# A hybrid decoder step on one core: the first burst of cached keys, the turn of v and the last norm chain change places

## What is computed

```python
h = rms_norm(x, norm_mix_pre[l])
u = h @ w_in[l]
hq, hf, hi, hgate, dq, dk, dv, g_hg, g_da = jnp.split(u, IN_SPLIT_POINTS, axis=-1)
...
o_hg, s_new = hgrn2_recurrence(hq, hf, hi, lb, s0)        # 8 heads, 128 x 128 states
o_hg = rms_norm(o_hg.astype(x.dtype), hg_norm_w[l]) * jax.nn.silu(hgate)
y_hg = o_hg.reshape(b, L, HG_WIDTH) @ w_branch_hg[l]
...
o_da = diff_attend(q, k_all, v_all, q_pos, k_pos, rel_bias_table, lam)   # 2 softmax maps a head
o_da = rms_norm(o_da.astype(x.dtype), da_subln_w[l]) * (1.0 - lam_init)
y_da = o_da.reshape(b, L, DA_WIDTH) @ w_branch_da[l]
mixed = (jax.nn.sigmoid(g_hg) * y_hg + jax.nn.sigmoid(g_da) * y_da) @ w_out[l]
```

## Time and profile before

| what | value |
|---|---|
| median of three runs | 1884.2 us |
| profiled execution, its own time | 1886.4 us |
| span of that execution | 1884.9 us |
| PE, ACT, DVE, POOL busy | 99%, 43%, 57%, 7% |
| stretch of the eight rounds | from about 185 us to about 805 us of the span |
| DMA, mean over the span | 236 GB/s; 304 to 383 GB/s in the page's slices of the rounds |
| granted TensorE clock, mean | 0.998 |

### The profile page before, as it was taken

One profiled execution on the slowest core, in us unless ns is written; L12 is line 12 of the kernel. 1 busy time (PEld: TensorE's weight loads), 2 busy tenths in 40 slices (PEclk: granted clock), 3 DMA queues, 4 the chain that ended last, 5 costly groups with the idle time before them and its releaser, 6 DMA issues.

```text
span 1884.9 us, 39626 instructions
## 1 busy us (share of the span) xinstructions
PE 1863.8 (99%) x15318; PEld 1772.6 (94%) x15318; DVE 1069.2 (57%) x1440; ACT 811.3 (43%) x1075; POOL 133.0 (7%) x172
## 2 busy tenths in 40 slices
PE   9999999999999999899999999999999999999998
PEld 9999888888888888699999999999999999999998
DVE  8443667566665676565547754544554445545555
ACT  6333535435444354454445433333333334445454
POOL 1023121011110110100000000000000000000000
PEclk9999999999999999999999999999999999999999
DMA  8877989989999999777544555445454454544541
GB/s 317 182 257 228 375 338 357 383 342 368 352 362 371 371 369 351 304 277 249 189 154 148 164 160 160 153 154 178 157 165 152 155 173 157 165 158 155 168 156 57
DMA packets 125183, 444.38 MB, mean 236 GB/s; under 512 B 15749, under 2 KB 19861, under 8 KB 125056
## 3 DMA queue, kind: packets, MB, share of 16 engines
q1 hardware_dynamic: 112720, 402.31, 59.7%
q0 software_dynamic: 11168, 39.72, 7.2%
q10 hardware_dynamic: 1232, 1.47, 0.2%
HBM read 423.50 MB, written 22.54 MB: 237 GB/s over the span
## 4 chain that ended last, share of the span: by engine, by line
PE 94%; DMA 2%; DVE 2%; issue 1%; ACT 1%; POOL 0%; ACTq 0%; DVEq 0%; SPq 0%; POOLq 0%
PE ps L447 49%; PE ps L436 6%; PE ps L438 6%; PE ps L437 6%; PE ps L1871 5%; PE ps L1873 5%; PE ps L1872 5%; PE ps L979 3%; PE ps L1008 3%; PE ps L1513 3%; DMA raw<-w_in 1%; DMA gates<-uT 0%; DMA uT<-stage 0%; DVE w_lo L372 0%; PE ps L752 0%
## 5 line engine op out<-in xcount | busy, mean ns | idle before, releaser
L372 DVE TENSOR_TENSOR w_lo<-raw,w_hi 128x1024 fp32r<-128x1024 f32 x416 | 510.8, 1243 | 453.7 <-ACT w_hi L367 240.3
L367 ACT ACTIVATE w_hi<-raw 128x1024 fp32r<-128x1024 f32 x236 | 245.8, 1055 | 363.8 <-PE ps L447 302.1
L1871 PE MATMUL ps<-hid_hi,w_hi 128*128 128x320 f32 x680 | 203.4, 299 | 0.0
L1872 PE MATMUL ps<-hid_hi,w_lo 128*128 128x320 f32 x680 | 203.3, 299 | 0.0
L1873 PE MATMUL ps<-hid_lo,w_hi 128*128 128x320 f32 x680 | 203.3, 299 | 0.0
L395 ACT ACTIVATE w_hi<-raw 128x1024 fp32r<-128x1024 f32 x124 | 128.0, 1051 | 148.2 <-DMA raw<-w_in 134.1
L447 PE MATMUL ps<-x_hi,w_hi 128*128 128x320 f32 x1200 | 191.0, 303 | 0.1
L447 PEld LDWEIGHTS ps<-x_hi,w_hi 128*128 128x128 f32 x1200 | 169.3, 189 | 10.9 <-issue 7.2
L447 PE MATMUL ps<-x_hi,w_lo 128*128 128x320 f32 x1136 | 177.5, 299 | 0.0
L447 PE MATMUL ps<-x_lo,w_hi 128*128 128x320 f32 x1072 | 167.5, 299 | 0.0
L447 PEld LDWEIGHTS ps<-x_hi,w_lo 128*128 128x128 f32 x1136 | 161.9, 189 | 0.0
(11 more groups left out here) (365 smaller groups left out, 3102.9 us busy)
## 6 DMA issues: line engine op xcount, KB each, us to landing
raw<-w_in SPq DMA_DIRECT2D x176, 512.0 KB, 8.2
raw<-w_up SPq DMA_DIRECT2D x176, 512.0 KB, 3.5
raw<-ck SPq DMA_DIRECT2D x128, 512.0 KB, 6.4
raw<-cv SPq DMA_DIRECT2D x128, 512.0 KB, 7.0
raw<-w_dn SPq DMA_DIRECT2D x88, 512.0 KB, 3.5
raw<-w_out SPq DMA_DIRECT2D x32, 512.0 KB, 4.3
uT<-stage POOLq DMA_DIRECT2D x14, 640.0 KB, 7.9
raw<-w_hg SPq DMA_DIRECT2D x16, 512.0 KB, 5.9
```

The costliest lines, as they stand in the source:

```text
L367: act.activation(w_hi[slot % HALVES][:, :], raw[slot][:, :], ACT.Copy).then_inc(hi_ready, 1)
L372: dve.tensor_tensor(w_lo[half][:, :], raw[slot][:, :], w_hi[half][:, :].bitcast(F32), ALU.subtract).then_inc(lo_ready, 1)
L1871: pe.matmul(ps[:, m, 0:T], wh[:, c], xh, **dict(add, start=q == 0))
L1872: pe.matmul(ps[:, m, 0:T], wl[:, c], xh, **add)
```

## The change

The key pages of the first burst come directly behind A0 in `ROUND`, ahead of A1, and PE takes the burst directly behind `new_scores`. v of the next head is turned at the end of a round, behind `turn_back`, and its copy on ACT (`tok`) stands there too. The banks of prompt scores, of v and of the turned probabilities are exchanged: scores in banks 4 and 6, v in 5, `pd_t` in 4. So "i_t" now waits for "s", "pd_t" for "st2", and the second burst no longer for `pdt`. In the last round ACT's "sq" waits for the head's output and `ds_s` and stands ahead of D2 hi; POOL's sum ("ss") stands ahead of the stores of the states; "rt" stands directly behind D2 hi; DVE reads the last gate set (L554) ahead of D1 lo.

```diff
-ROUND = (items("A", 0, 2) + BURSTS[0] + items("A", 2, 6) + BURSTS[1] + items("A", 6, 8) + items("D", 0, 4)
+ROUND = (items("A", 0, 1) + BURSTS[0] + items("A", 1, 6) + BURSTS[1] + items("A", 6, 8) + items("D", 0, 4)
...
-        k_pool = Steps(sem("k_pool"), "zero ss", 1)
+        k_pool = Steps(sem("k_pool"), "ss", 1)
...
+        def act_v(act, h):
+            h_act.begin()
+            act.wait_ge(h_pe.sem, h_pe.at(h, "vk"))
+            h_act.done(act.activation(v_tok[:, :, :], ps[:, 5, 0:2 * P].rearrange("p (c d) -> p c d", c=2), ACT.Copy), "tok")
...
             if q == 1:
-                h_act.begin()
                 act.wait_ge(set_out, 4 * hg_set(h) + 2)
                 act.wait_ge(h_pool.sem, h_pool.last(h - 1))
                 h_act.done(act.activation(kin[:, :], x[:, 1, :], ACT.Sigmoid), "ef")
-                act.wait_ge(h_pe.sem, h_pe.at(h, "vk"))
-                h_act.done(act.activation(v_tok[:, :, :], ps[:, 6, 0:2 * P].rearrange("p (c d) -> p c d", c=2),
-                                          ACT.Copy), "tok")
...
+        def v_by_token(pe, h):
+            h_pe.begin()
+            pe.wait_ge(head_landed, HEAD_LOADS * (h + 1))
+            pe.sem_inc(passed, 1)
+            for j in range(2):
+                ins = pe.transpose(ps[:, 5, j * P:(j + 1) * P], mv[:, j * P:(j + 1) * P], ident[:, :])
+            h_pe.done(ins, "vk")
...
                 pe.wait_ge(h_vec.sem, h_vec.at(h, "i_smp"))
-                pe.wait_ge(h_act.sem, h_act.at(h, "tok"))
+                pe.wait_ge(h_vec.sem, h_vec.at(h, "s"))
                 h_pe.done(to_tokens(x[:, 2, :], i_smp[:, :, :, :], 6), "i_t")
...
             if q == 5:
-                pe.wait_ge(h_vec.sem, h_vec.at(h, "aT"))
+                pe.wait_ge(h_vec.sem, h_vec.at(h, "st2"))
                 for j in range(3):
-                    ins = pe.transpose(ps[:, 5, j * P:(j + 1) * P], pd[:, j * P:(j + 1) * P], ident[:, :])
+                    ins = pe.transpose(ps[:, 4, j * P:(j + 1) * P], pd[:, j * P:(j + 1) * P], ident[:, :])
...
             elif what == "sq":
-                act.wait_ge(h_vec.sem, h_vec.last(r))
+                act.wait_ge(h_vec.sem, h_vec.at(r, "o"))
+                act.wait_ge(h_pe.sem, h_pe.last(r))
...
-                k_vec.done(dve.tensor_tensor(s_all[:, :, HALF:], ps[:, 4:6, 3 * P:3 * P + NQ], near[:, :, PAGE:], ALU.add), "new")
+                for m in range(2):
+                    ins = dve.tensor_tensor(s_all[:, m, HALF:], ps[:, 4 + 2 * m, 3 * P:3 * P + NQ], near[:, m, PAGE:], ALU.add)
+                k_vec.done(ins, "new")
...
                 pe.wait_ge(k_act.sem, k_act.at(r, "g0"))
-                pe.wait_ge(h_act.sem, h_act.at(r, "pdt"))
                 pe.sem_inc(passed, 1)
             else:
-                pe.wait_ge(h_vec.sem, h_vec.at(r, "s"))
+                pe.wait_ge(h_act.sem, h_act.at(r, "tok"))
...
             round_hi(act, r + 1, "A", 0)
             act_pages(act, r, "o")
+            act_v(act, r + 1)
...
             act_pages(act, r, "p")
+            act_pages(act, r, "sq")
             round_hi(act, r, "D", 2)
-            act_pages(act, r, "sq")
+            act_pages(act, r, "rt")
             act_pages(act, r, "p0")
             act_pages(act, r, "pn")
             round_hi(act, r, "D", 3)
-            act_pages(act, r, "rt")
...
             round_lo(dve, r, "D", 0)
+            read_set(dve, gate_set(r), 1, SETS_U + 2 + r)
             round_lo(dve, r, "D", 1)
-            read_set(dve, gate_set(r), 1, SETS_U + 2 + r)
...
-                if q in (1, 5):
+                if q in (0, 5):
                     scores(pe, r, q // 4)
...
             turn_back(pe, r)
+            v_by_token(pe, r + 1)
...
             store_set(pool, gate_set(r), 1, GATE + 4 * r)
+            k_pool.begin()
+            if isinstance(r, int):
+                square_sums(pool, r)
             pool_head(pool, r)
```

More of the change, by code:

```diff
@@ L301, in build @@
         h_pe = Steps(sem("h_pe"), "vk scores i_t kd_t a ds pd_t o_s0 pv o ds_s", 1)
-        h_act = Steps(sem("h_act"), "ef tok lg eG p i_tok kd_tok pdt i_smp o_att", 1)
+        h_act = Steps(sem("h_act"), "tok ef lg eG p i_tok kd_tok pdt i_smp o_att", 1)
         h_vec = Steps(sem("h_vec"), "i_smp fg kin s max nmax G Gd qk qkd rc rcl pd2 pd aT st1 mid st2 own o s_three s_new", 1)
@@ L310, in build @@
         v_n_landed = sem("v_n_landed")
+        v_n_zero = sem("v_n_zero")
         k_pe = Steps(sem("k_pe"), "new h0 s0 h1 s1", 1)
-        k_pool = Steps(sem("k_pool"), "zero ss", 1)
+        k_pool = Steps(sem("k_pool"), "ss", 1)
         k_act = Steps(sem("k_act"), "q silu g0 g1 p sq rt rt_da", 1)
@@ L593, in act_head @@
                 act.wait_ge(h_pe.sem, h_pe.at(h, "pd_t"))
-                h_act.done(act.activation(pdt[:, :, :], ps[:, 5, 0:3 * P].rearrange("p (c d) -> p c d", c=3),
+                h_act.done(act.activation(pdt[:, :, :], ps[:, 4, 0:3 * P].rearrange("p (c d) -> p c d", c=3),
                                           ACT.Copy), "pdt")
@@ L635, in vec_head @@
                     close = mb[:, m, :]
[L636 removed]
+                    dve.scalar_tensor_tensor(s_at[:, m, 0:P], ps[:, 4 + 2 * m, 0:P], SCALE, close[:, P:2 * P],
                                              ALU.mult, ALU.add)
[L638 removed]
+                    ins = dve.scalar_tensor_tensor(s_at[:, m, P:3 * P], ps[:, 4 + 2 * m, P:3 * P], SCALE, close,
                                              ALU.mult, ALU.add)
@@ L730, in pe_head @@
             if q == 0:
-                h_pe.begin()
-                pe.wait_ge(head_landed, HEAD_LOADS * (h + 1))
                 pe.wait_ge(v_vec.sem, v_vec.last(h - 1))
-                for j in range(2):
-                    ins = pe.transpose(ps[:, 6, j * P:(j + 1) * P], mv[:, j * P:(j + 1) * P], ident[:, :])
-                h_pe.done(ins, "vk")
                 for m in range(2):
                     own_q, own_k = mq[DH * m:DH * m + DH, :], mk[DH * m:DH * m + DH, :]
-                    pe.matmul(ps[:, 4 + m, 0:P], own_q[:, 0:P], own_k[:, 0:P], start=True, stop=True)
-                    ins = pe.matmul(ps[:, 4 + m, P:3 * P], own_q[:, P:SEQ], own_k[:, 0:SEQ], start=True, stop=True)
+                    pe.matmul(ps[:, 4 + 2 * m, 0:P], own_q[:, 0:P], own_k[:, 0:P], start=True, stop=True)
+                    ins = pe.matmul(ps[:, 4 + 2 * m, P:3 * P], own_q[:, P:SEQ], own_k[:, 0:SEQ], start=True, stop=True)
                 h_pe.done(ins, "scores")
@@ L952, in new_scores @@
                         h, own, rows = 2 * j + e, slice(DH * m, DH * m + DH), own_rows(1, e)
-                        ins = pe.matmul(ps[32 * j:32 * j + 32, 4 + m, 3 * P:3 * P + NQ], q_rows[own, h, rows], k_own[own, h, :],
+                        ins = pe.matmul(ps[32 * j:32 * j + 32, 4 + 2 * m, 3 * P:3 * P + NQ], q_rows[own, h, rows], k_own[own, h, :],
                                         start=e == 0, stop=e == 1)
@@ L1173, in pe_last, with square_sums @@
             turn_back(pe, r)
+        def square_sums(pool, r):
+            pool.wait_ge(k_act.sem, k_act.at(r, "sq"))
+            pool.sem_inc(passed, 1)
+            k_pool.done(pool.partition_all_reduce(sq_all[:, :], n_sq[:, :], channels=P, reduce_op=bass.bass_isa.ReduceOp.add), "ss")
         def pool_round(pool, r):
@@ L1182, in pool_round @@
             pool.sem_inc(stage_free, 1)
-            k_pool.begin()
-            k_pool.done(pool.memset(v_new[:, :], 0.0), "zero")
-            pool.wait_ge(k_pool.sem, k_pool.at(r, "zero"))
+            pool.memset(v_new[:, :], 0.0).then_inc(v_n_zero, 1)
+            pool.wait_ge(v_n_zero, r + 1)
             pool.sem_inc(passed, 1)
@@ L1188, in pool_round @@
                 bass.ds(r, 1)].rearrange("a q d -> (a q) d")).then_inc(v_n_landed, 16)
-            pool.wait_ge(k_act.sem, k_act.at(r, "sq"))
-            pool.sem_inc(passed, 1)
-            k_pool.done(pool.partition_all_reduce(sq_all[:, :], n_sq[:, :], channels=P, reduce_op=bass.bass_isa.ReduceOp.add), "ss")
+            if not isinstance(r, int):
+                square_sums(pool, r)
             pool.wait_ge(head_stored, HEAD_STORES * (r + 1))
@@ L1991, in _ @@
             act.wait_ge(new_v_stored, 16)
+            act.wait_ge(bias_stored, 16)
+            act_v(act, 0)
             with act.Fori(0, LAST) as r:
@@ L2113, in _ @@
             pe.wait_ge(new_v_kept, 2)
+            v_by_token(pe, 0)
             with pe.Fori(0, LAST) as r:
@@ L2121, in _ @@
             pool.sem_inc(h_pool.sem, 1)
-            pool.sem_inc(k_pool.sem, 2)
+            pool.sem_inc(k_pool.sem, 1)
             pool.sem_inc(stage_free, 2)
```

## The result

| | before | after |
|---|---|---|
| median | 1884.18 us (1882.97 to 1884.62, 6 runs) | 1891.36 us (1889.85 to 1892.97, 6 runs) |
| profiled execution, its own time | 1886.44 us | 1889.85 us |
| its span | 1884.9 us | 1888.3 us |

The changed kernel is **slower by 0.38%**: ratio 1.0038, 95% interval 1.0028 to 1.0049. The forecast was 1887.4 us, its range 1876 to 1892: the median lies inside the range, 4.0 us above the forecast. In microseconds the two medians are 7.2 apart, with an interval of 5.3 to 9.2, where the forecast had 3.2.

The account below looks back on a forecast made before the run. PE was taken to bound the kernel, busy 1863.8 of 1884.9 us. Rounds +11.4 - 1.5 - 0.5 = +9.4 us, last round -6.2, sum +3.2: 1887.4 us against the median of 1884.2, range 1876 to 1892.

Parts of the forecast that it names:

- t + 15.5 us: Rounds 1 to 7: `ds` can start 15.5 us after A1 hi's start t, through ACT's and DVE's in-order work.
- The term of 11.4 us: Later `ds` summed over rounds 1 to 7: 11.4 us lost, bounds 0 and 15; round 1 worst, round 3 best.
- The first rival: Rounds 1 to 7: chain behind A1 hidden, rounds cost only PE's own, total 1876.4 us; chance 0.22.
- the burst's join: First burst behind `new_scores`: one entry to and one return from small tiles saved, 0.30 us a round.
- the rival "saves nothing": First burst: one block saves nothing, `ds` absorbs it in rounds 1 to 7, 0.3 us lost: 1887.7; no chance given.
- the second burst: Second burst of each round: its wait for ACT's `pdt` goes, 0.21 us a round, 1.5 over rounds 1 to 7.
- the last round: Last round: earlier norm roots cut the wait ahead of D3; `turn_back` moves from 803.61 to 797.4, -6.2 us.
- the rival that POOL holds the chain: Last round: the norm chain is held by POOL, +2.5 us, total 1889.9; chance 0.08.
- the prediction's last estimate: Last round on DVE: a small sum of the division would be held by POOL's sum for about 1.1 us.
- The slower rival: First value page: sum over partitions catches D4's remainder in four more rounds, +6.6 us, total 1894; chance 0.10.
- v a round ahead: v's transposes behind `turn_back`, ACT's copy ahead of A1 hi: costs 0, or 0.4 us if uncovered.
- "s" for "i_t": Bank exchange: "i_t" waits for "s", which ends near 435.2, before PE arrives at 436.1; no cost unless late.

Follow-up runs that it names:

- the two pairs: Kernel before and changed kernel, both unedited, each profiled twice and compared execution by execution; the parts of the shift sum to +6.0 and +5.9 us.
- the halving: Changed kernel with four of a burst's eight key waits ahead of it and four ahead of its second half: 1890.42 us, ratio 1.0044 to the kernel before.
- all repairs: Changed kernel with the head's elementwise work ahead of A1's split, key waits by half, rows' copy between branch granules: 1877.33 us, 1876.67 us when repeated.

## Why the prediction was right, and where it fell short

**Right: what decides.** The prediction picked the load order, worked out that A1's late landing makes `ds` late by the elementwise chain on ACT and DVE, and set t + 15.5 us. Rounds 1 to 7 of both profiles, 14 in all, lie between 15.28 and 15.50. The term of 11.4 us measured 12.1 and 11.1. Only the sum agrees so well: single rounds lie between +1.0 and +2.6 us, and the same round differs by up to 0.9 us between the two executions, so that round 3, forecast as the best with 1.3, lost 2.3 in the first. Moving the head's work off that chain took the median from 1891.36 to 1881.58 and in the profile 7.8 us from these seven rounds: shown by experiment. The first rival, the chain hidden, is out. Its price was wrong too: with the chain out of the way the kernel took 1881.58 us and not 1876.4, for the reason that follows.

**Wrong by size: the burst's join, -0.30 us a round.** In round 0, where nothing behind is late, the step from `new_scores` to "kd_t" costs +0.42 and +0.41 us in the two pairs. I counted an entry and a return saved, and nothing for PE's queue. Joining saves 0.17 us behind "i_t" (0.20 to the burst before, 0.03 to A2 now) and 0.02 of the return (1.19 us before, 1.17 now, behind the transposes): 0.19 and not 0.30. Against it, the burst starts 0.61 us later behind `new_scores` than A1 did (0.88 against 0.27). `new_scores` is 32 matmuls of 8 columns and over in 0.27 us, which covers few of the burst's eight key waits; A1 and the transposes had covered them all (0.20 us from the last transpose to the burst). With four waits the cost is +0.2 instead of +0.4 us in rounds 0 to 6: shown by the halving in three profiles. What the rest of the 0.61 us is made of, no run here shows. Only round 0 pays in the changed kernel (+0.8 against the forecast, with the 0.1 of its second burst); elsewhere `ds` absorbs it, as the rival "saves nothing" said.

**Wrong by size: the second burst, -0.21 us a round.** It measured 0.06 to 0.12 in the first pair (0.28 in round 7). The row "<- ACT pd, 0.2" names what PE waited for last; right beneath lie the key waits, shown by the halving. That is some 0.6 us over seven rounds. Another 0.3 is that behind a wait for `kd_tok` the stretch from `ds` to "pd_t" takes 7.07 us instead of 7.02. Together the term is +0.8 to +1.0 us off.

**Right: the last round**, -6.2 us by way of ACT's second branch granule. It stood at 796.26 before and at 805.52 after; the rounds had moved by 9.3, so it moved by 0.0 of its own where I had -0.4, and `turn_back` gained 6.0 us in the first pair, 4.9 in the second (before's second execution was itself quicker there). Alone it gave 4.7 us in the median, with an interval of 2.8 to 6.8. The sum over partitions began (782.15) as D1's remainder ended, which took its usual 1.24 us; the rival that POOL holds the chain is out. A small addition of the division (L928) ran inside the sum and took 0.28 us instead of 0.16, so it was held for 0.1 us where the prediction's last estimate had about 1.1.

**Right by luck: the profiled execution.** The forecast for it was 1889.6 us, and it took 1889.85; the spans differ by 3.4 us where the forecast had 3.2. The table shows what that is made of: +6.0 of the change, and -3.4 of stalls at the first value page that did not come back. The same program a second time had 1.4 us of them instead of 3.3. In the medians, where such chance evens out, the 3.2 us stand against 7.2. So what the forecast lacked is 2.7 to 2.8 us by the table (join 0.8, second burst 0.8 to 1.0, and the rest in landings or in the last round), and 1.2 us or so that no row places.

**The slower rival**, the sum catching D4's remainder in four more rounds, did not come: waits for `p_keys` 0 and 2 times. **v a round ahead** and **"s" for "i_t"** cost nothing, as said: no wait of PE names `v_tok` or `s_at` in either profile.

## What to carry over

When a load moves back in the order, find the first instruction on each in-order engine that waits for it and walk the work behind it to the next consumer: here a load set back by eight slots cost some 1.7 us a round through ACT and DVE, and taking independent work out from behind it gave 1.1 of that back. Count the semaphore waits on PE's queue where the matmuls ahead are short, above all in a loop, and spread them over the work that needs them. Price a wait of PE by the distance between two starts, not by the idle time in the view, which was a quarter too small here (6.4 against 8.5 us). Compare a change of a few tenths of a percent by two profiles of each kernel, since one of them can hold several microseconds of stalls that are nobody's.

## What the runs showed of the hardware

- **Semaphore waits that hold nothing up by themselves cost time on PE's queue when the work before them is short**: in the looped rounds four fewer gave 0.2 us back, at the first burst (0.85 to 0.65 us) and at the second (0.75 to 0.56). In the round that is written out, eight and four waits gave the same at the second burst (0.57 and 0.56).
- **The granted clock fell behind short idle times in some rounds only**: with A1 loaded first it fell to half behind 1.85 and 1.83 us of waiting for keys (rounds 3 and 5) and stayed at full behind 1.81, 1.98 and 1.85 (rounds 2, 6 and 7), and the 2.57 us ahead of `turn_back` left it at full in the changed kernel's profile. No run here separates what the difference is.
- **The sum over partitions holds DVE's remainder, an operation with two SBUF inputs, until 2.3 us behind the sum's start, and not for its whole 3.55 us.** In the kernel before, remainders that began 1.26 and 1.56 us behind the start took 2.30 and 2.00 us instead of 1.2, and one that began 2.66 us behind it took 1.23. One that began up to 0.33 us ahead of the sum was held as well (3.88 us, all repairs, round 0; 3.70 and 3.75 in the kernel before). From 0.37 us ahead on it was not, and the sum took longer instead: 4.32, 4.01 and 3.89 us behind remainders that began 0.37, 0.68 and 0.80 us ahead, in the changed kernel's two profiles. So the prediction's remark that the one that began first was held is true of the small leads only.
- **A stall differs between executions of one program**: 3.3 and 1.4 us, 0 and 2.5 us in sum, on one core.
